# A hybrid SSD/HGRN2/MoE decoder layer: inputs laid out by the host in load order, the first projection group in four pieces

## What is computed

```
h   = rmsnorm(x) * norm_mix_w
z, xbc, dt, q, f, v, g = split(h @ w_in)                # 6672 columns
xbc = silu(causal_conv4(xbc, state_conv)); conv state returned
y   = ssd(xs, dt, B, C, state_ssm) (+ d_skip*xs), * silu(z), group rms norm
o   = hgrn2(q, f, v, state_hgrn), rms norm, * silu(g)
x   = x + concat(y, o) @ w_out
x   = x + MoE(rmsnorm(x))                                # 16 experts, 1 group of 4, top 2
x   = x + sigmoid(rmsnorm(x) @ w_ple_gate) * (p @ w_ple_proj)
out = rmsnorm(x); new ssm, conv and hgrn states
```

## Time and profile before

| | us |
|---|---|
| timed runs | 649.36, 652.38, 654.05 |
| median | 652.38 |
| span of the profiled execution | 645.5 |
| PE busy in it | 597.3 (93%) |
| DVE, ACT, POOL busy | 292.0, 175.6, 80.8 |

### The profile page before, as it was taken

One profiled execution on the slowest core, in us unless ns is written; L12 is line 12 of the kernel. 1 busy time (PEld: TensorE's weight loads), 2 busy tenths in 40 slices (PEclk: granted clock), 3 DMA queues, 4 the chain that ended last, 5 costly groups with the idle time before them and its releaser, 6 DMA issues.

```text
span 645.5 us, 9639 instructions
## 1 busy us (share of the span) xinstructions
PE 597.3 (93%) x3802; PEld 392.3 (61%) x3802; DVE 292.0 (45%) x943; ACT 175.6 (27%) x421; POOL 80.8 (13%) x101
## 2 busy tenths in 40 slices
PE   4999999999998999999999699999988887999996
PEld 2788888788587887788786333333332332334684
DVE  2388459568559999454211731100110101116574
ACT  3122427621543433636101411111110100100333
POOL 4200023321011112110000021121111101000000
PEclk9999999999999999999999889999998987989999
DMA  9833354999332776728998599999999999998001
GB/s 262 290 131 131 130 201 143 362 332 334 137 102 72 255 225 204 260 96 306 367 393 355 210 415 382 425 425 427 423 425 424 424 422 421 427 410 319 2 1 67
DMA packets 45705, 179.69 MB, mean 278 GB/s; under 512 B 3932, under 2 KB 12576, under 8 KB 37201
## 3 DMA queue, kind: packets, MB, share of 16 engines
q1 hardware_dynamic: 35136, 147.21, 58.4%
q0 software_dynamic: 10000, 30.67, 14.8%
q10 hardware_dynamic: 520, 1.15, 0.5%
HBM read 167.65 MB, written 17.39 MB: 287 GB/s over the span
## 4 chain that ended last, share of the span: by engine, by line
PE 71%; DMA 20%; DVE 4%; ACT 2%; issue 2%; SPq 1%; DVEq 0%; ACTq 0%
PE bank L919 26%; DMA arena<-in_w_exp_up 15%; PE bank L1380 12%; PE bank L1173 9%; PE bank L1418 6%; DMA arena<-in_w_in 5%; PE bank L1516 4%; DVE arena L1843 1%; PE bank L1391 1%; PE bank L1016 1%; PE bank L1131 1%; PE bank L1077 1%; PE bank L1471 1%; PE bank L950 1%; PE bank L1194 1%
## 5 line engine op out<-in xcount | busy, mean ns | idle before, releaser
L919 PE MATMUL bank<-hT,arena 128*128 128x264 f32 x768 | 175.3, 387 | 1.5 <-DMA arena<-in_w_in 1.5
L919 PEld LDWEIGHTS bank<-hT,arena 128*128 128x128 f32 x768 | 144.4, 190 | 27.4 <-issue 2.3
L1380 PE MATMUL bank<-arena,hT 128*64 128x512 f32 x512 | 123.5, 632 | 15.7 <-DMA arena<-in_w_exp_up 10.5
L1380 PEld LDWEIGHTS bank<-arena,hT 128*64 128x64 f32 x512 | 39.5, 145 | 91.0 <-issue 89.3
L1851 DVE SCALAR_TENSOR_TENSOR hT<-hT,sq,bank 128x256 f32<-128x256 f32 x16 | 7.7, 480 | 137.3 <-ACT hT L1766 137.3
L1843 DVE TENSOR_TENSOR arena<-arena 128x256 f32<-128x256 f32 (+7 forms) x146 | 60.4, 458 | 16.3 <-ACT arena L1658 9.9
L1418 PE MATMUL bank<-arena,sq 128*64 128x512 f32 x256 | 58.5, 598 | 0.9 <-ACT sq L1771 0.9
L1173 PE MATMUL bank<-arena 128*128 128x264 f32 x256 | 58.1, 387 | 1.3 <-issue 1.3
L1173 PEld LDWEIGHTS bank<-arena 128*128 128x128 f32 x256 | 48.3, 190 | 10.4 <-issue 2.3
L1766 ACT ACTIVATE hT<-bank 128x256 f32<-128x256 f32 x16 | 6.1, 383 | 141.8 <-PE bank L1380 141.8
L1588 ACT ACTIVATE arena<-bank 128x264 f32<-128x264 f32 x40 | 15.5, 389 | 105.3 <-PE bank L919 105.3
(11 more groups left out here) (313 smaller groups left out, 643.4 us busy)
## 6 DMA issues: line engine op xcount, KB each, us to landing
arena<-in_w_exp_down SPq DMA_DIRECT2D x16, 2048.0 KB, 19.4
arena<-in_w_exp_gate SPq DMA_DIRECT2D x15, 2048.0 KB, 22.5
arena<-in_w_exp_up SPq DMA_DIRECT2D x15, 2048.0 KB, 27.4
arena<-in_w_in SPq DMA_DIRECT2D x13, 2048.0 KB, 11.8
out<-arena POOLq DMA_DIRECT2D x18, 512.0 KB, 6.4
arena<-in_w_out SPq DMA_DIRECT2D x4, 2048.0 KB, 9.8
arena<-in_state_ssm POOLq DMA_DIRECT2D x8, 512.0 KB, 8.7
arena<-in_state_hgrn POOLq DMA_DIRECT2D x8, 512.0 KB, 4.8
```

What stands on the lines that cost most here:

```text
L919: last = mm(ps[:, 0:T], w[:, k, j * P:(j + 1) * P], x, start=(k == 0), stop=(k == KT - 1))
L1380: last = mm(bank[p][r, :].rearrange("p (w f) -> p w f", w=2), xgT[:, p, k % 4, CAP * (k // 4):CAP * (k // 4) + CAP], gu[:, :, k, FF // 2 * ...
```

## The change

The host arranges the inputs so that each load reads one contiguous run per partition, and turns the outputs back. Nothing of the arithmetic on tokens changes.

- x arrives transposed, in two halves of 4 x 264 columns, directly in `xT`; group 0 of `w_in` arrives in four tiles of 512 KB, each with a semaphore of its own. The order on SP is: x half 0, tile 0, x half 1, tile 1, first part of `K`, tiles 2 and 3, rest of `K`, group 1 (without the wait on `ld_prm`).
- Groups 1 to 12, `w_out`, `w_ple_gate`, `w_ple_proj` and the states are contiguous for each partition (16 KB, 8 KB or 4 KB).
- Parameters come as columns in four loads on ACT's queue; all small loads of POOL's queue go.
- The transposes of lines 900, 906, 929, 937, 941 and 990 go, and the copies by ACT and DVE that belong to them. The `tail` is made by three copies on POOL, in column form, and stored from there.
- POOL's first state loads wait for group 1 in place of group 0.
- `p` is loaded transposed; the two transposing jobs go, and the eight others stand two turns earlier (`PLE_JOBS` 10 to 8).

```diff
         @block.sync
+            for i in range(2):
+                eng.dma_start(xT[:, 4 * i:4 * i + 4].rearrange("p k t -> p (k t)"), ins["x"][i]).then_inc(ld_x[i], 16)
+                eng.dma_start(W[:, 0, 1024 * i:1024 * i + 1024], ins["w_in_first"][i]).then_inc(ld_w0[i], 16)
             eng.dma_start(K[:, 0:K_AFTER], consts[:, 0:K_AFTER]).then_inc(ld_k, 16)
-            for i, (t0, n) in enumerate(TOK):
-                src = ins["x_prompt"][0, t0:t0 + n] if i < 2 else ins["x_sample"][:, 0]
-                eng.dma_start(xtok[0:n, i], src).then_inc(ld_x[i], 16)
...
-            for g, c in enumerate(starts):
-                if g == 1:
-                    eng.dma_start(K[:, K_AFTER:K_N], consts[:, K_AFTER:K_N]).then_inc(ld_kr, 16)
-                    eng.wait_ge(ld_prm, 16 * 8)
+            for i in range(2, 4):
+                eng.dma_start(W[:, 0, 1024 * i:1024 * i + 1024], ins["w_in_first"][i]).then_inc(ld_w0[i], 16)
+            eng.dma_start(K[:, K_AFTER:K_N], consts[:, K_AFTER:K_N]).then_inc(ld_kr, 16)
+            for g in range(1, GROUPS):
                 if g >= 2:
                     eng.wait_ge(a_full, ja["proj", 4 * g - 5] + 1)
-                eng.dma_start(W[:, g % 2].rearrange("p (k c) -> p k c", k=KT), w_in[:, :, c:c + 512]
-                              ).then_inc(w_slot[g % 2], 16)
+                eng.dma_start(W[:, g % 2], ins["w_in_rest"][g - 1]).then_inc(w_slot[g % 2], 16)
...
         @block.gpsimd
-            eng.wait_ge(w_slot[0], 16)
+            eng.wait_ge(w_slot[1], 16)
             for b in range(4):
                 s1_load(b)
 
+            eng.wait_ge(ld_cv, 16)
+            eng.tensor_copy(tail_s[:, :, :, 0:2], convu[:, :, :, 1:3]).then_inc(tail_made, 1)
+            eng.wait_ge(a_took, ja["proj", CT - 1] + 1)
+            eng.tensor_copy(tail_s[:, :, :, 2], PR[:, 0:CT, NP_:T]).then_inc(tail_made, 1)
+            eng.tensor_copy(tail_p, PR[:, 0:CT, NP_ - 3:NP_]).then_inc(tail_made, 1)
+            eng.wait_ge(tail_made, 3)
+            eng.dma_start(outs[6], tail[:, 0:NCV]).then_inc(tail_out, 16)
+            eng.dma_start(outs[3], tail[:, NCV:NCV + 3 * CT]).then_inc(tail_out, 16)
             eng.wait_ge(v_took, jv["bcs"] + 1)
...
         @block.tensor
             def proj_group(g):
-                eng.wait_ge(w_slot[g % 2], 16 * (g // 2 + 1))
+                if g:
+                    eng.wait_ge(w_slot[g % 2], filled(g))
                 for j in range(4):
                     n = ja["proj", 4 * g]
+                    if g == 0:
+                        eng.wait_ge(ld_w0[j], 16)
                     proj_tile(g % 2, j, n, n, g)
...
         @block.scalar
+            eng.dma_start(first_smalls, ins["first"]).then_inc(ld_first, 16)
+            eng.dma_start(prm[:, :], ins["columns"]).then_inc(ld_prm, 16)
+            eng.dma_start(convu_all, ins["state_conv"]).then_inc(ld_cv, 16)
+            eng.dma_start(wrb[:, :], ins["router"]).then_inc(ld_r, 16)
...
             for ft in range(KT):
-                activation(xT[:, ft], full("xT", ft)[:, 0:T], ACT.Copy).then_inc(a_took, 1)
-            for ft in range(KT):
-                square(ft, a_took, ft + 1)
+                square(ft, ld_x[ft // 4], 16)
...
         @block.vector
+            eng.wait_ge(tail_made, 1)
             for g in range(G):
                 tt(CBm[:, g], full("cb", g)[:, 0:384], K[:, K_CAUSAL:K_CAUSAL + 384]).then_inc(v_took, 1)
...
-            eng.wait_ge(a_took, ja["tail", 2] + 1)
+            eng.wait_ge(tail_made, 3)
             link(tt(PR[:, 0:KT, NP_:T].rearrange("p f b -> p b f"), yss, DX, ALU.add))
```

More of the change, by code:

```diff
@@ L170, in make_jobs @@
     a.add("w")
-    for i in range(3):
-        a.add("tail", i)
     for tt in range(2):
@@ L446, in build @@
         lbe = small(3, HH)
[L447 to L449 removed]
+        wrb = sb("wrb", [P, KT * 20 + 20])
+        wr = wrb[:, 0:KT * 20].rearrange("p (k c) -> p k c", k=KT)
+        rb = wrb[:, KT * 20:KT * 20 + 20]
         rt = sb("rt", [P, 3, 20])
@@ L465, in build @@
         v_full, v_took = sem("v_full"), sem("v_took")
-        ld_k, ld_kr, ld_mix = sem("ld_k"), sem("ld_kr"), sem("ld_mix")
+        ld_k, ld_kr, ld_first = sem("ld_k"), sem("ld_kr"), sem("ld_first")
         table_in, raw_ready, first_sum = sem("table_in"), sem("raw_ready"), sem("first_sum")
-        ld_x = [sem(f"ld_x{i}") for i in range(3)]
+        ld_x = [sem(f"ld_x{i}") for i in range(2)]
+        ld_w0 = [sem(f"ld_w0_{i}") for i in range(4)]
+        tail_made = sem("tail_made")
         tail_out, st_out = sem("tail_out"), sem("st_out")
-        ld_p, ld_prm = sem("ld_p"), sem("ld_prm")
-        ld_s = sem("ld_s")
+        ld_cv, ld_prm = sem("ld_cv"), sem("ld_prm")
         ld_r = sem("ld_r")
@@ L986, in _ @@
             mm(ps[:, 2 * H:3 * H], after, av[:, 0], start=True, stop=True).then_inc(a_full, 1)
-            for i in range(3):
-                ps = open_a("tail", i)
-                for j in range(4):
-                    last = nc.tensor.transpose(ps[0:11, j * P:(j + 1) * P], PR[:, 4 * i + j, NP_ - 3:T], ident)
-                last.then_inc(a_full, 1)
             for tt in range(2):
@@ L1426, in ple_job @@
                     eng.wait_ge(ple_took, n)
-                if n < 2:
-                    eng.wait_ge(ld_pp, 48)
-                    for i, (t0, rows) in enumerate(TOK):
-                        last = nc.tensor.transpose(ps[:, t0:t0 + rows], ptok[0:rows, i, n * P:(n + 1) * P],
-                                                   ident[0:rows, 0:rows])
-                else:
-                    c = n - 2
-                    for k in range(2):
-                        last = mm(ps[:, 0:T], wpp[:, k, c * P:(c + 1) * P], pT[:, k], start=(k == 0), stop=(k == 1))
+                if n == 0:
+                    eng.wait_ge(ld_pp, 32)
+                for k in range(2):
+                    last = mm(ps[:, 0:T], wpp[:, k, n * P:(n + 1) * P], pT[:, k], start=(k == 0), stop=(k == 1))
                 last.then_inc(ple_full, 1)
@@ L1613, in _ @@
             activation(rest, full("w")[:, 2 * H:3 * H], ACT.Copy).then_inc(a_took, 1)
-            for i in range(3):
-                activation(tail[0:11, i * 512:(i + 1) * 512], full("tail", i)[0:11, :], ACT.Copy).then_inc(a_took, 1)
             def f_gates(h):
@@ L2522 @@
     arrays, ins = {}, {}
-    for name in _INS:
-        x = np.ascontiguousarray(inputs[name])
+    for name, x in laid_out({k: np.asarray(v) for k, v in inputs.items()}).items():
+        x = np.ascontiguousarray(x)
         arrays[f"in_{name}"] = x
@@ L2531 @@
     r = run_bass_kernel_spmd(nc, [arrays], core_ids=[0])
-    return tuple(r.results[0][f"out_{i}"] for i in range(len(_OUTS)))
+    return tuple(np.ascontiguousarray(a) for a in returned([r.results[0][f"out_{i}"] for i in range(len(_OUTS))]))
```

196 lines of the change are left out of this document (83 added, 113 removed).

## The result

| us | before | after |
|---|---|---|
| timed runs (this comparison) | 648.68, 649.36, 652.38, 654.05 | 633.74, 633.77, 634.29, 636.96 |
| median | 650.87 | 634.03 |
| ratio of the medians, 95% interval | | 0.974 (0.970 to 0.978) |
| span of the profiled execution | 645.5 | 631.9 |

A forecast was written before the change was run, and what follows sets the result against it. PE, busy 93% of the span, bounds the kernel up to the expert part, then the saturated weight stream. Terms 12.4 + 1.3 + 1.5 + 1.2 + 0.8 = 17.2 us, so 652.4 - 17.2 = 635.2 us, range 629 to 643.

The forecast's parts named there:

- The start: PE's first projections: first record at 6.9 us, group 1 at 24.4 instead of 36.86; gain 12.4 us (8.6 to 16.5).
- The first rival: Start loads: pieces share the engines and don't land in order; start gain falls by 5.7, time 640.9 us; chance 0.12.
- Tail transposes: PE's transposes for the tail go, saving 1.3 us.
- Late `w_in` groups: PE's waits on two late `w_in` groups vanish through longer runs: 1.5 us (0 to 1.5).
- The slower rival: Groups with 16 KB runs land late; from 16.1 us landing the gain is gone, at 17.6 time 669; chance 0.03.
- DVE's state update: PE's wait for DVE shrinks because the SSD state store gets 4 KB runs: 0.8 us (0 to 1.5).
- the rival by which DVE's chain keeps its own pace: Little gain: at 190 to 203 us PE waits for DVE, about 9 us remains, 643 us; chance 0.08.
- `w_out` group 2: PE's wait for this load, the one with the shortest runs (1 KB), goes: 1.2 us (0 to 1.26).
- What PE gains before 360 us moves the start of the saturated stream and with it the end.: Expert weights: the stream waits for the routing, so all 17.2 us gained ahead of 360 us reaches the end.
- the stretch from group 1 to the routing 5 us shorter: Sign of a right forecast: PE's time between group 1's begin and the routing falls by 5 us.
- Costed at nothing: POOL's three copies, DVE's `tail_made` waits, later states, two fewer expert jobs (under 1 us) and ACT's parameter loads add nothing.

The follow-up runs named there:

- experiment 2: The changed kernel with POOL's ten small loads put back at the start, fetching unused data into spare room: 636.56 us.
- experiment 1: The changed kernel with group 0 of `w_in` in one 2 MB load behind both halves of x: 636.50 us; repeated, median 638.63 us, ratio to before 0.980.
- experiment 3: The changed kernel with `w_in` groups 1 to 12 and `w_out` read in the short runs of before (2 KB and 1 KB): 638.76 us.
- experiment 4: The changed kernel with the SSD and HGRN2 states loaded and stored in 512 B runs again: 638.55 us.
- experiment 7: The changed kernel with `w_out` group 2 loaded in two 1 MB halves, each with its own semaphore: 634.39 us.
- experiment 6: The changed kernel with the 24 narrow `dt` matmuls spread behind group 2's first three tiles: 630.62 us; repeated, median 631.83 us, ratio to before 0.970.
- experiment 8: The changed kernel with spread `dt` matmuls, `w_out` group 2 and first weight tile in halves, two ACT parameter loads later: median 628.40 us, ratio to before 0.963.
- experiment 5: The kernel before, with POOL's ten small loads held until group 0 has landed: 653.45 us (before in the same comparison: 653.06).

## Why the prediction was right, and where it was not

The forecast holds, and the mechanisms are those it named, but for one term (`w_out`) and for the clock, which the sum left out. Term by term, trace against trace:

- **The start, 12.4 predicted, 12.7 measured.** The first record came at 6.32 (6.9 predicted), x half 1 at 8.2 (9.8). The pace that was carried over from before's 5.41 to 8.25 us was itself slowed by POOL's loads, as experiment 2 shows. Group 0 took 17.85 (17.5): the first two tiles 10.45 in place of 9.9. Carrying over the slow first tile was right, in a start without transposes too. The first rival is refuted by experiment 1.
- **Tail transposes, 1.3 and 1.3** (11.1 to 12.4 in the table).
- **Late `w_in` groups, 1.5 predicted, 2.0 measured** (12.4 to 14.4). The median from issue to landing fell by 16%, inside the "few per cent to 20%"; experiment 3 shows the wait coming back with the short runs. The slower rival needed a landing time of 16.1 us in every group; the most was 14.7.
- **DVE's state update, 0.8 and 1.1** (14.4 to 15.5). The store went from 3.91 us to 2.9, and DVE's wait for it from 1.45 to 0.31; experiment 4 shows the way from the runs to PE's wait. So the rival by which DVE's chain keeps its own pace and takes the gain back is refuted: the gain grows across it.
- **`w_out` group 2, 1.2 predicted, 0.3 measured.** This step failed. I took the wait for an effect of "the shortest runs, 1 KB". With runs of 16 KB PE still begins 8.05 us after the issue (298.59 to 306.64, before 8.4), and with short runs experiment 3 waited 1.2. In the traces with long runs and the load in one piece the wait is 0.8 to 1.0 us. What sets it is the time at which the load can be issued, a slot's release, against the time of a 2 MB load; experiment 7 takes the wait away with a smaller first piece.
- **"What PE gains before 360 us moves the start of the saturated stream and with it the end."** It moved the start: 15.2 us at the second expert. To the end it held only within some 2 us: 2.2 are lost in the second expert and little comes back. In experiment 1 the same code of the experts was 3.4 us shorter, so this part varies from execution to execution; over four runs 3.8 (by the ratios) to 4.6 us (by the medians) of 4.5 reached the end.
- **What was not in the sum at all:** 1.7 us at the lower clock in group 3. The sum took every matmul that stays for a matmul that costs the same. The stretch is there in all eight executions with an earlier start and the block of narrow `dt` products in one piece, and in none of the three with the block spread (experiments 6 and 8). That the earlier start brings it about is not shown: there is one trace of before, and that is an execution with a high clock. Because of this stretch and of the `w_out` term the sign "the stretch from group 1 to the routing 5 us shorter" came out at 2.5: 325.43 us before (36.86 to 362.29), 322.96 after (24.17 to 347.13).
- **Costed at nothing, and so it was:** POOL's copies take 0.3 to 0.4 us each, and POOL is idle for 19.06 us ahead of the store of `bc_rows`. Not quite nothing is the order of the jobs of the per-layer input, which cost 0.5 us in the second expert's turn. In POOL's timeline of the changed kernel:

```profile
53.36 0.32 POOL L696 COPY arena<-arena 128x96 f32<-128x96 f32 x1 [30.64 <-ACT arena L1526]
...
74.34 0.55 POOL L702 DMA_DIRECT2D bc_rows<-arena  x1 [19.06 <-DVE arena L1890]
```

The terms ahead of the experts make 12.7 + 1.3 + 2.0 + 1.1 + 0.3 = 17.4, where the sum had 17.2. Less the 1.7 lost in group 3 that is 15.7 (15.6 in the table at `w_out`), and less the loss in the experts 13.6. That the median nevertheless fell by 16.8 lies in the executions: the profiled one of before was a short one. The forecast's nearness to the median is thus partly luck; by the traces the sum was 3.6 us too large, mostly for the two places at the lower clock. Whether a typical execution of before has such stretches too, so that they cancel in the median, is open.

## What to carry to other kernels

At the start, give the first consumer pieces of its own size in the order in which it wants them, and keep small scattered loads out of that stretch: up to group 1 the pieces were worth 4.5 us and the absence of the ten small loads 2.2. Loads behind it that have no slack can take a gain at the start back, some 4 us with one late group in experiment 3, so lengthen their runs in the same step. A block of narrow matmuls among wide ones can cost more than its own time; look at the granted clock right behind it, and spread it between wide tiles.

## What the runs showed of the hardware that was not expected

- In the changed kernel and in experiments 1 (two executions) to 5 and 7, all with the `dt` block in one piece, a stretch at clock 0.5 begins within the last part of that block or right behind it, 3.4 to 6.8 us long; group 3 then took 15.7 to 17.1 us (16.12 in the changed kernel and in experiment 5), against 14.44 in before. PE is shown busy through the whole block. In the one trace of before the same block is followed by 1.00. What spares it there is open, and so is whether other executions of before are spared.
- Waits of 1.2 to 3.6 us by PE were followed by such a stretch in experiments 1, 3, 4, 5 and 7; others of that size, like the 1.63 us of before, were not. One wait for ACT shows both: after 1.19 us of it the clock fell to 0.50 in experiments 4 and 7, and after the same 1.19 us it stayed at 1.00 in the changed kernel. What decides was not tried.
- The first two tiles of group 0 took 8.94 to 10.45 us in nine executions of kernels that start PE between 5.7 and 11.7 us, against 7.3 for the next two, at a granted clock of 1.00 in the rows. Neither transposes ahead of them nor a later begin changes that much. PE's pace there, 6 records in 2 us (10 to 12 us above), is the pace that the rows show at 0.50 (58 to 60 us). A lower clock that the rows do not show would fit, but no run shows it; the cause is open.
- With small loads of POOL's queue under way the DMA share reads 1.21 at 181 GB/s; without them 1.03 at 419. A full share is not a full rate.
